# Two attention units' scores issued together on two row groups of the array, and the grouped-query heads reordered to make such pairs

## The reference, cut to what matters

```
A  na    4 heads of 64, keys: 512 latent (bias table, mask) + 128 cached context
B  swa   4 query heads of 64 on 2 key/value heads, band mask, a learned sink logit in the softmax, rotary
D  df    4 heads, each with two maps of 32 channels; a = softmax(s1) - lambda * softmax(s2), then a @ v
```

```
s = einsum('..qhd,..khd->..hqk', q, k) * scale (+ bias)
p = softmax(s) ;  o = p @ v          (df: o = (p1 - lam * p2) @ v)
```

## Time and profile before

| | us |
|---|---|
| median of 3 runs | 2949.17 |
| lowest, highest | 2943.51, 2962.62 |
| span of the profiled execution | 2935.3 |
| PE busy in it | 2626.5 (89%) |
| DVE, ACT, POOL busy in it | 984.1, 574.5, 1223.0 |

### The profile page before, as it was taken

One profiled execution on the slowest core, in us unless ns is written; L12 is line 12 of the kernel. 1 busy time (PEld: TensorE's weight loads), 2 busy tenths in 40 slices (PEclk: granted clock), 3 DMA queues, 4 the chain that ended last, 5 costly groups with the idle time before them and its releaser, 6 DMA issues.

```text
span 2935.3 us, 42778 instructions
## 1 busy us (share of the span) xinstructions
PE 2626.5 (89%) x16100; PEld 2380.8 (81%) x16100; DVE 984.1 (34%) x1545; ACT 574.5 (20%) x936; POOL 1223.0 (42%) x500
## 2 busy tenths in 40 slices
PE   6998996888888899999979999968888898999998
PEld 5985675777778799999969766667777787999998
DVE  4024455444445411111230254554444453111112
ACT  3103444111111211001020143431111112100000
POOL 1531003443444466566525300034434444665663
PEclk8997898989889999999989978978888899999999
DMA  5221011222221122222332211112222211221232
GB/s 202 72 74 51 29 62 40 81 81 96 80 80 57 57 71 82 69 71 75 115 106 79 79 42 36 46 56 81 89 83 85 82 54 57 72 88 63 71 107 102
DMA packets 60511, 222.09 MB, mean 76 GB/s; under 512 B 6800, under 2 KB 8464, under 8 KB 60048
## 3 DMA queue, kind: packets, MB, share of 16 engines
q1 hardware_dynamic: 60432, 221.12, 22.4%
HBM read 217.16 MB, written 3.93 MB: 75 GB/s over the span
## 4 chain that ended last, share of the span: by engine, by line
PE 81%; DVE 12%; issue 3%; ACT 2%; DMA 1%; DVEq 0%; SPq 0%; ACTq 0%
PE lp L415 59%; DVE small_lo L1075 5%; PE lp L506 5%; PE ss L491 5%; PE ss L444 3%; DVE tmp L1089 2%; PE lp L518 2%; DMA small<-ada 1%; DVE tmp L1085 1%; PE lp L536 1%; PE ss L492 1%; PE lp L582 1%; DVE mg L864 1%; PE ss L487 1%; PE ss L576 0%
## 5 line engine op out<-in xcount | busy, mean ns | idle before, releaser
L415 PEld LDWEIGHTS lp<-H,wr 128*128 128x128 f32 x9792 | 1516.9, 196 | 98.6 <-DVE H L877 41.6
L415 PE MATMUL lp<-H,wr 128*128 128x320 f32 x9792 | 1534.2, 318 | 69.8 <-DVE H L877 39.7
L375 POOL TENSOR_TENSOR wr<-wst,con 128x1024 fp32r<-128x1024 f32 (+2 forms) x236 | 497.5, 2108 | 1229.7 <-PE lp L415 1063.8
L377 POOL TENSOR_TENSOR wr<-wst,wr 128x1024 fp32r<-128x1024 f32 (+2 forms) x236 | 690.0, 2924 | 18.5
L415 PE MATMUL lp<-G,wr 128*128 128x320 f32 x2112 | 310.4, 308 | 0.0
L415 PEld LDWEIGHTS lp<-G,wr 128*128 128x128 f32 x2112 | 309.9, 188 | 0.0
L1075 DVE TENSOR_TENSOR small_lo<-small,small_hi 128x1024 fp32r<-128x1024 f32 x64 | 208.6, 3260 | 4.4 <-ACT small_hi L796 1.9
L1138 DVE TENSOR_TENSOR tmp<-lp,tmp 128x640 f32<-128x640 f32 x44 | 36.3, 825 | 495.8 <-PE lp L415 495.8
L444 PE MATMUL ss<-small_hi,cds 128*4 128x512 f32 x128 | 65.0, 508 | 139.4 <-DVE small_lo L1075 139.0
L805 ACT ACTIVATE tmp<-lp,vc 128x640 f32<-128x640 f32 x64 | 50.9, 795 | 587.2 <-PE lp L415 587.1
L1085 DVE TENSOR_TENSOR tmp<-lp,tmp 128x640 f32<-128x640 f32 x48 | 39.6, 825 | 374.6 <-PE lp L415 374.6
(11 more groups left out here) (139 smaller groups left out, 1880.1 us busy)
## 6 DMA issues: line engine op xcount, KB each, us to landing
wst<-wff SPq DMA_DIRECT2D x88, 512.0 KB, 3.3
wst<-wgu SPq DMA_DIRECT2D x64, 640.0 KB, 4.5
small<-adb SPq DMA_DIRECT2D x64, 512.0 KB, 3.3
wst<-win SPq DMA_DIRECT2D x36, 512.0 KB, 3.3
bt<-bias SPq DMA_DIRECT2D x40, 320.0 KB, 3.2
adae<-ada SPq DMA_DIRECT2D x12, 1024.0 KB, 6.2
wst<-wfa SPq DMA_DIRECT2D x16, 768.0 KB, 4.3
wst<-wfb SPq DMA_DIRECT2D x16, 640.0 KB, 3.8
```

Of the source, the lines that this page charges most:

```text
L375: pool.tensor_tensor(wr[:, s, 0, 0:w], wst[:, s, 0:w], con[:, C_ONE:C_ONE + 1].to_broadcast([P, w]), ALU.mult).then_inc(w_hi[s], 1)
L377: pool.tensor_tensor(wr[:, s, 1, 0:w], wst[:, s, 0:w], wr[:, s, 0, 0:w].bitcast(F32), ALU.subtract).then_inc(w_lo[s], 1)
L415: mm = pe.matmul(out[:, h, 0:TH], w[wi], act[:, ai, k, h * TH:(h + 1) * TH], start=first and i == 0, stop=last and i == 2)
```

## The change

In `attend`, the scores are no longer issued one unit per iteration but two units every second iteration. `free` is the old wait of one unit; at an even u both are waited for, then the 512-column products of u and u+1 are issued, then their 128-column products, each of the latter reporting its unit as ready. P@V and T of both iterations follow as before. Units u and u+1 lie on different row groups: na heads 0 and 1, the maps of a df head, and, after the reordering of `UNITS_T`, swa heads 0 and 2, then 1 and 3, which lie in one chunk of `qs` on partitions 0-63 and 64-127. Code of VectorE and ScalarE is unchanged except for that order of the swa heads.

```diff
-UNITS_T = [...] + [("swa", h, 0) for h in range(4)] + \
+UNITS_T = [...] + [("swa", h, 0) for h in (0, 2, 1, 3)] + \
...
+                def free(u):
+                    if u >= 2:
+                        pt_, (k_, _, _) = seq[u - 2]
+                        if (k_ == "na" and pt_ is not None) or k_ == "swa":
+                            pe.wait_ge(s_pre, u0 + u - 1)
+                        else:
+                            pe.wait_ge(s_exp, u0 + u - 1)
...
                 for u in range(len(seq) + 5):
-                    if u < len(seq):
...
-                        out = sflat[u % 2]
...
-                            pe.matmul(out[:, 0:NLAT], q, qk[p0:p0 + n, kc, NCTX:T], start=True, stop=True)
-                            mm = pe.matmul(out[:, NLAT:KEYS], q, ck[p0:p0 + n, cc, :], start=True, stop=True)
-                        mm.then_inc(s_ready, 1)
+                    if u < len(seq) and u % 2 == 0:
+                        free(u)
+                        free(u + 1)
+                        for e in range(2):
+                            t, unit = seq[u + e]
+                            qc, kc, cc, p = place(*unit)
+                            if t is None:
+                                pe.matmul(sflat[e][:, NLAT:KEYS], qk[p, qc, 0:NCTX], qk[p, kc, 0:NCTX], start=True, stop=True)\
+                                    .then_inc(s_ready, 1)
                             else:
+                                pe.matmul(sflat[e][:, 0:NLAT], qs[p, t, qc, :], qk[p, kc, NCTX:T], start=True, stop=True)
+                        for e in range(2):
+                            t, unit = seq[u + e]
+                            qc, kc, cc, p = place(*unit)
+                            if t is not None:
+                                pe.matmul(sflat[e][:, NLAT:KEYS], qs[p, t, qc, :], ck[p, cc, :], start=True, stop=True)\
+                                    .then_inc(s_ready, 1)
```

More of the change, by code:

```diff
@@ L68 @@
 LOCAL = {"PER_V": 195, "PER_ATT": 64}
-UNITS_T = [("na", h, 0) for h in range(4)] + [("swa", h, 0) for h in range(4)] + \
+UNITS_T = [("na", h, 0) for h in range(4)] + [("swa", h, 0) for h in (0, 2, 1, 3)] + \
           [("df", h, c) for h in range(4) for c in range(2)]
@@ L465, in attend @@
                 turn, combs = plan(seq)
-                for u in range(len(seq) + 5):
-                    if u < len(seq):
[L468 to L473, removed]
-                            else:
[L475 to L484, removed]
-                        out = sflat[u % 2]
[L486 to L490, removed]
-                            pe.matmul(out[:, 0:NLAT], q, qk[p0:p0 + n, kc, NCTX:T], start=True, stop=True)
-                            mm = pe.matmul(out[:, NLAT:KEYS], q, ck[p0:p0 + n, cc, :], start=True, stop=True)
-                        mm.then_inc(s_ready, 1)
@@ new lines, in free, with place @@
+                def free(u):
[5 more added lines that the diff above has]
+                            pe.wait_ge(s_exp, u0 + u - 1)
+                def place(kind, h, c):
+                    if kind == "na":
+                        return NA_Q + h // 2, NA_K + h // 2, h // 2, slice(h % 2 * 64, h % 2 * 64 + 64)
+                    if kind == "swa":
+                        return SWA_Q + h % 2, SWA_K, 2, slice(h // 2 * 64, h // 2 * 64 + 64)
+                    p0 = h % 2 * 64 + c * 32
+                    return DIFF_Q + h // 2, DIFF_K + h // 2, 3 + h // 2, slice(p0, p0 + 32)
```

## The result

The median went from 2949.17 us to **2973.24 us** (15 runs each): ratio 1.0079, 95% interval 1.0055 to 1.0104. The changed kernel is slower by 0.8%; the forecast was 3015. 2973 is the time that rival 1 had, but the clock was not kept, as its condition asks.

The account below looks back on a forecast made before the run. PE was taken to bound the attention, which lies on the chain. Lost cover at an unchanged clock (+24 us) and the lower clock (net +44) made +68 on the profiled span, 2935 to 3003; median 3015, range 2960 to 3065.

Parts of the forecast that it names:

- rival 1: Clock stays at full rate, so only the +24 us of the attention walk counts: 2973 us; chance 20%.
- Concurrent scores: Score products of two units run side by side on two row groups: 1.28 us a pair, TensorE alone saving 81 us.
- Rivals 3 and 4: 32-row groups do not run side by side, 3046 us (12%); no overlap in the steady part at all, 3085 us (5%).
- The copy of T before P@V: Steady na/swa pair: the next P@V waits 1.49 us instead of 0.64; pair 5.85 us against 6.28 before.
- First df head behind swa: Units 8 and 9: scores behind wait for the second exponential, after a late copy of T; 7.6 us against 6.28, +1.3.
- Later heads: Third and fourth df heads: both maxima and the combination between them delay the next scores; 5.52 us against 4.55, +0.97 each.
- Next tile's first pair: First pair of a tile after df heads, at full clock: 4.95 us against 4.55, +0.4.
- The sum at a kept clock: Four latent sequences at +5.2 us each, +21, plus the context pass: +24 us at an unchanged clock.
- The clock: Idle PE in df stretches lowers the granted clock, lasting into the next tile: 54 us less 10 already paid, net +44.
- rival 2: Copy and exponential chains hidden, so only PE's work counts and 81 us are saved: 2868 us; chance 5%.
- From span to median: The median was taken as 13.9 us above the profiled span, turning 3003 us into 3017, said as 3015.

Follow-up runs that it names:

- both orders: The change plus T ahead of P@V on TensorE and both maxima ahead of the combination on VectorE: 2884.36 us, ratio 0.9780 to before; repeated, 2879.26 us.
- the fillers: The change plus matmuls that nothing reads in idle TensorE time, ahead of waiting P@V and behind df P@V: 2969.50 us, ratio 1.0088 to before.
- the second experiment: The change with T ahead of P@V in each iteration on TensorE: 2944.72 us, ratio 0.9994 to the kernel before.

## Why the prediction was wrong

- *Concurrent scores:* right, for 64 and for 32 rows (1.13 us for four records). PE's busy time in the latent part fell by 51 us, at a granted clock of 0.82 and 0.86; with both orders, at 0.92, it fell by 93. Rivals 3 and 4 are out.
- *The copy of T before P@V:* right, 5.86 against 5.85. T ahead of P@V took it away and 25 to 28 us with it.
- *First df head behind swa:* right, 7.50 against 7.6. *Later heads:* right, 5.53 against 5.52. Putting the two maxima first took the wait of the later heads away and 29 to 31 us with it. *Second head:* 5.72 against 5.8 at the full clock.
- *Next tile's first pair:* 5.98 against 4.95, as it begins at the lower clock (scores of 2.08); with the fillers, at the full clock, 5.02. *Its second:* 4.70 against 4.62. *Context tile:* +3.5 for both layers against +3.
- *The sum at a kept clock:* +24 forecast. The profiled attention grew by 34.8, 9 of which the fillers gave back, so some 26 are left, which fits. The medians differ by 24.1, but they hold a cost of the clock that this sum leaves out, so the agreement to 0.1 us is in part luck.
- **The clock: this step failed.** "I expect the lower clock in most df stretches, lasting into the next tile", priced at 44 us net. The price of a head at it was right (6.99 against 6.95 in the second experiment), and the drops came. But the prediction let each last through two heads and into two pairs of the next tile, 8 us at each change of tile. Inside the sequences the rows show 3.4 and 6.8 us; only in 4 of 8 tiles did a drop touch the second head (7.15 instead of 5.72), and where a head waits for VectorE and ScalarE a short drop fits into PE's idle time (the P@V at 308.74 took 2.08 instead of 1.16, and its head still 5.54). The fillers, which bring the clock to that of before or above, gave back 9 us in the profile and 4 in the median, which the intervals do not tell from nothing: about 9 or less in place of the 44. The one stretch of before at the lower clock for 17.1 us was an end of a sequence; the prediction took its length for the middle of one too. At the ends it came nearer: from the last tile's first df head, the second sequences end 7.8 and 7.5 us later than before, and the fillers gave back 3 of that in each.
- *The other side* (rival 2, PE's work is all that counts): not for this change, but its number was the right one to look at. With both covers restored the saving is 65 to 71 us by the medians and 50 between the profiled executions, against its 81; the shorter steps of T and P@V are in that too.
- *From span to median:* the 13.9 us added were for the most part the quick profiled execution. Harmless here, since the sum was made on differences.

## What to carry to other kernels

Work that an engine does while another engine prepares its next input hides that wait: it is cover. Before two steps are issued together, write down for each wait in the loop what stood in front of it, and put something else there: here the transposes ahead of the value products, and both maxima ahead of the combination. The same overlap made this kernel 0.8% slower without that and 2.2% faster with it. A drop of the clock must be priced with its length in that very place, and only where the engine has no idle time to absorb it; the length is hard to know ahead, as it was 6.8 us at a tile's end in the change and 13.4 with T ahead of P@V.

## What the runs showed of the hardware that was not expected

- fp32 score products of two units run fully side by side on different row groups, on 64 and on 32 rows alike: four 512-column records in 1.13 us, one unit's two in 1.12.
- The two row groups one after the other, with PE busy 87%, had a granted clock of 0.66; side by side, busy 77%, 0.82 and 0.86; in the kernel before, busy 96%, 0.89 and 0.90. PE's busy share alone does not tell what the clock will do.
- The order of transposes and value products matters little where nothing is waited for: 3.09 against 3.13 us a unit.
